# Two layers of a hybrid diffusion backbone on one core: loops written out as straight code, and two modulation jobs of the last layer left out

## What is computed

```python
def trunk_layer(x, m, latent, ...):
    h = rmsnorm(x, g[0]) * (1 + m[:, :, 0, 1]) + m[:, :, 0, 0]
    x = x + 0.5 * m[:, :, 0, 2] * rmsnorm(swiglu(h, wg[0], wu[0], wd[0]), g[1])
    h = rmsnorm(x, g[2]) * (1 + m[:, :, 1, 1]) + m[:, :, 1, 0]
    p = h @ w_in                       # Fourier | Hyena | q, k, v
    ...
    y = jnp.concatenate([y_f, y_h, y_a], axis=-1) @ w_out
    x = x + m[:, :, 1, 2] * rmsnorm(y, g[3])
    h = rmsnorm(x, g[4]) * (1 + m[:, :, 2, 1]) + m[:, :, 2, 0]
    x = x + 0.5 * m[:, :, 2, 2] * rmsnorm(swiglu(h, wg[1], wu[1], wd[1]), g[5])
```

## Time and profile before

| | |
|---|---|
| median of 3 runs | 1707.59 us (1707.35 to 1709.22) |
| span of the profiled execution, first to last instruction | 1706.8 us |
| mean granted TensorE clock | 0.985 |
| busy: PE, PEld | 1607.5 us, 1462.8 us |
| busy: DVE, ACT, POOL | 899.6 us, 765.5 us, 17.8 us |
| read from memory, written | 260.73 MB, 6.55 MB |

### The profile page before, as it was taken

One profiled execution on the slowest core, in us unless ns is written; L12 is line 12 of the kernel. 1 busy time (PEld: TensorE's weight loads), 2 busy tenths in 40 slices (PEclk: granted clock), 3 DMA queues, 4 the chain that ended last, 5 costly groups with the idle time before them and its releaser, 6 DMA issues.

```text
span 1706.8 us, 26956 instructions
## 1 busy us (share of the span) xinstructions
PE 1607.5 (94%) x9434; PEld 1462.8 (86%) x9434; DVE 899.6 (53%) x1597; ACT 765.5 (45%) x1176; POOL 17.8 (1%) x39
## 2 busy tenths in 40 slices
PE   6799999998988899999989999999898889999996
PEld 2399989996966699989979998999696669998996
DVE  5655544336685655544336554533667565554433
ACT  2355544325535555543255544432552555554332
POOL 0000000000000000000000000000000000000000
PEclk9999999999999999999999999999999999999998
DMA  6833685345501433474343368534550144337331
GB/s 232 333 107 125 249 294 182 130 159 182 181 1 38 173 123 123 137 282 138 129 167 100 124 247 293 191 124 165 181 181 1 36 163 130 124 126 298 132 124 65
DMA packets 70613, 268.20 MB, mean 157 GB/s; under 512 B 9387, under 2 KB 10444, under 8 KB 69900
## 3 DMA queue, kind: packets, MB, share of 16 engines
q1 hardware_dynamic: 67164, 248.96, 41.7%
q0 software_dynamic: 3376, 18.35, 2.8%
HBM read 260.73 MB, written 6.55 MB: 157 GB/s over the span
## 4 chain that ended last, share of the span: by engine, by line
PE 87%; DVE 6%; issue 3%; DMA 2%; ACT 2%; POOL 0%; DVEq 0%; SPq 0%; ACTq 0%; POOLq 0%
PE bank L529 26%; PE bank L531 25%; PE bank L530 25%; PE bank L538 4%; PE bank L867 1%; PE bank L829 1%; DVE y L1271 1%; DMA w_m<-w_mod 1%; DVE rstd L1266 1%; PE bank L753 1%; PE bank L617 1%; DMA f_cst<-tneg 1%; DVE sb_s L1457 1%; ACT prob_t L1068 1%; PE bank L856 1%
## 5 line engine op out<-in xcount | busy, mean ns | idle before, releaser
L1207 DVE TENSOR_TENSOR w_lo<-w_raw,w_hi 128x1024 fp32r<-128x1024 f32 (+2 forms) x288 | 373.6, 1297 | 527.5 <-ACT w_hi L927 526.6
L529 PE MATMUL bank<-h_hi,w_hi 128*128 128x386 f32 (+1 forms) x1760 | 606.3, 344 | 1.3 <-DVE w_lo L1207 0.8
L531 PE MATMUL bank<-h_hi,w_lo 128*128 128x386 f32 (+1 forms) x1760 | 596.1, 339 | 0.0
L530 PE MATMUL bank<-h_lo,w_hi 128*128 128x386 f32 (+1 forms) x1760 | 595.5, 338 | 0.0
L927 ACT ACTIVATE w_hi<-w_raw 128x1024 fp32r<-128x1024 f32 (+2 forms) x288 | 322.1, 1118 | 528.2 <-PE bank L531 527.6
L529 PEld LDWEIGHTS bank<-h_hi,w_hi 128*128 128x128 f32 x1760 | 332.0, 189 | 20.9 <-issue 14.0
L530 PEld LDWEIGHTS bank<-h_lo,w_hi 128*128 128x128 f32 x1760 | 332.8, 189 | 1.2
L531 PEld LDWEIGHTS bank<-h_hi,w_lo 128*128 128x128 f32 x1760 | 332.3, 189 | 0.0
L530 PE MATMUL bank<-hid_lo,w_hi 128*128 128x384 f32 x704 | 238.4, 339 | 0.0
L529 PE MATMUL bank<-hid_hi,w_hi 128*128 128x384 f32 x704 | 238.4, 339 | 0.0
L531 PE MATMUL bank<-hid_hi,w_lo 128*128 128x384 f32 x704 | 238.4, 339 | 0.0
(11 more groups left out here) (194 smaller groups left out, 1123.5 us busy)
## 6 DMA issues: line engine op xcount, KB each, us to landing
w_raw<-w_gu SPq DMA_DIRECT2D x176, 512.0 KB, 3.3
w_m<-w_mod SPq DMA_DIRECT2D x160, 512.0 KB, 6.3
w_raw<-w_dn SPq DMA_DIRECT2D x64, 704.0 KB, 4.0
w_raw<-w_in SPq DMA_DIRECT2D x26, 512.0 KB, 3.4
w_raw<-w_out SPq DMA_DIRECT2D x16, 512.0 KB, 3.4
cst<-consts POOLq DMA_DIRECT2D x8, 688.0 KB, 5.9
spec<-f_spec POOLq DMA_DIRECT2D x2, 2304.0 KB, 8.2
spc<-spec POOLq DMA_DIRECT2D x8, 576.0 KB, 5.1
```

The source lines that it names most:

```text
L529: mm(out, w_hi[:, wn, c], rhs_hi, start=first, stop=False)
L530: mm(out, w_hi[:, wn, c], rhs_lo, start=False, stop=False)
L531: return mm(out, w_lo[s][:, c], rhs_hi, start=False, stop=last)
L1207: TT(w_lo[unit % RAW][:, 0:n], w_raw[unit % RAW][:, 0:n], w_hi[:, unit % HIS, 0:n], ALU.subtract).then_inc(unit_lo.sem, 1)
```

## The change

All `Fori` loops become Python loops, so that each engine's program is straight code; the numbers to wait for and the addresses become constants. The last layer's feed-forward 1 gets no modulation jobs (`jobs_in`), and its norm's job is turned ahead of round 10 instead of round 8, since `first` is 10 there. `coefs(layer + 1, 0)` is not called in the last layer, and the third layer's room in `mod`, `bmod` and `vec` goes, with the two loads that filled it.

```diff
+def jobs_in(layer, n):
+
+    return 0 if n and layer == DEPTH - 1 else JOBS[n]
 ...
 class Steps:
     def at(self, n):
-        return self.layer * self.per_layer + (self.base + n)
+        return n
 ...
-        mod = sb("mod", [P, DEPTH + 1, NMOD * KT * 2])
-        bmod = sb("bmod", [P, (DEPTH + 1) * NMOD * KT])
+        mod = sb("mod", [P, DEPTH, NMOD * KT * 2])
+        bmod = sb("bmod", [P, DEPTH * NMOD * KT])
 ...
-                    sp.dma_start(vec[:, 0:DEPTH, :], vecs.rearrange("l p v -> p l v")).then_inc(vec_loaded.sem, 16)
-
-                    sp.dma_start(vec[:, DEPTH, :], vecs[DEPTH - 1]).then_inc(vec_loaded.sem, 16)
-                    sp.dma_start(bmod[:, 0:DEPTH * NMOD * KT], b_mod).then_inc(vec_loaded.sem, 16)
-                    sp.dma_start(bmod[:, DEPTH * NMOD * KT:],
-                                 b_mod[:, (DEPTH - 1) * NMOD * KT:]).then_inc(vec_loaded.sem, 16)
+                    sp.dma_start(vec[:, :, :], vecs.rearrange("l p v -> p l v")).then_inc(vec_loaded.sem, 16)
+                    sp.dma_start(bmod[:, :], b_mod).then_inc(vec_loaded.sem, 16)
 ...
-                with sp.Fori(1, first) as i:
+                for i in range(1, first):
                     gate_up(i)
-                gate_up(first, own=True)
-                with sp.Fori(first + 1, ROUNDS - 1) as i:
-                    gate_up(i, before=True, own=True)
-                gate_up(ROUNDS - 1, before=True)
+                for i in range(first, ROUNDS):
+                    gate_up(i, before=i > first, own=i < ROUNDS - 1)
 ...
             def ffn(layer, n):
-                first = ROUNDS - 1 - JOBS[n]
+                first = ROUNDS - 1 - jobs_in(layer, n)
 ...
-                with pe.Fori(1, first) as i:
+                for i in range(1, first):
                     body(i, False)
                 norm_job_turn(layer, 2 * n)
-                with pe.Fori(first, ROUNDS - 1) as i:
+                for i in range(first, ROUNDS - 1):
                     body(i, True)
 ...
-            with pe.Fori(0, DEPTH) as layer:
+            for layer in range(0, DEPTH):
                 ffn(layer, 0)
 ...
-                last = JOB_FFN[n] + JOBS[n] - 1
+                last = JOB_FFN[n] + jobs_in(layer, n) - 1
                 job_finish(layer * JL + (last + 3), layer * NMOD + (last + 2))
 ...
                 if n == 0:
                     coefs(layer, 1)
-                else:
+                elif layer + 1 < DEPTH:
                     coefs(layer + 1, 0)
```

More of the change, by code:

```diff
@@ L171, with __init__ @@
 class Steps:
-    def __init__(self, layer, per_layer, base=0):
-        self.layer, self.per_layer, self.base, self.n = layer, per_layer, base, 0
+    def __init__(self):
+        self.n = 0
     def step(self):
@@ L426, in round_job @@
                     else:
-                        job_loads(layer, i + (JOB_FFN[1] - first), DEPTH - 1, i - first, kts)
+                        job_loads(layer, i + (JOB_FFN[1] - first), layer + 1, i - first, kts)
                 def gate_up(i, before=False, own=False):
@@ L457, in _ @@
                 norm_loads(layer, 1, 1)
-                with sp.Fori(1, 3) as i:
+                for i in range(1, 3):
                     for u in range(4):
@@ L463, in _ @@
                     load_unit(layer, B_IN + 13 + j, w_in[layer, 13, :, a * P:b * P], (b - a) * P)
-                with sp.Fori(0, OUTT // 4) as i:
+                for i in range(0, OUTT // 4):
                     for u in range(4):
@@ L487, in _ @@
             pool.sem_inc(spec_free.sem, 1)
-            with pool.Fori(0, DEPTH) as layer:
+            for layer in range(0, DEPTH):
                 pool.wait_ge(spec_ready.sem, spec_ready.at(layer, 1))
@@ L699, in ffn @@
                     body(0, False)
-                with pe.Fori(1, first) as i:
+                for i in range(1, first):
                     body(i, False)
                 norm_job_turn(layer, 2 * n)
-                with pe.Fori(first, ROUNDS - 1) as i:
+                for i in range(first, ROUNDS - 1):
                     body(i, True)
                 body(ROUNDS - 1, False)
-                with pe.Fori(0, KT // 2) as i:
+                for i in range(0, KT // 2):
                     for u in range(4):
@@ L735, in project_in @@
                     tile_of(B_IN + u, u, 0, range(KT), True, True)
-                with pe.Fori(1, 3) as i:
+                for i in range(1, 3):
                     for u in range(4):
@@ L871, in project_out @@
             def project_out(layer):
-                with pe.Fori(0, OUTT // 4) as i:
+                for i in range(0, OUTT // 4):
                     for u in range(4):
@@ L907, in _ @@
             act.wait_ge(f_dec.sem, 1)
-            with act.Fori(0, DEPTH) as layer:
+            for layer in range(0, DEPTH):
                 act.wait_ge(f_hs.sem, f_hs.at(layer, 0))
@@ L981, in tile_steps @@
                       ACT.Copy).then_inc(hid_hi_done.sem, 1)
-                with act.Fori(0, ROUNDS - 1) as i:
+                for i in range(0, ROUNDS - 1):
                     tile_steps(i, 0)
@@ L1015, in centre @@
                       scale=vconv[:, 3 * i + 1:3 * i + 2]).then_inc(conv0.sem, 1)
-                with act.Fori(0, 2) as i:
+                for i in range(0, 2):
                     for u in range(4):
@@ L1124, in job_finish @@
                 TT(dst, src, bias.broadcast_to([P, 4, 2, 2]), ALU.add).then_inc(mod_ready.sem, 1)
-            ch = Steps(0, 0)
+            ch = Steps()
             for n in range(2):
@@ L1149, in _ @@
             STT(out=dec, in0=dec, scalar=-1.0, in1=dec, op0=ALU.mult, op1=ALU.max).then_inc(f_dec.sem, 1)
-            trace["dve_head"] = ch.n
-            with dve.Fori(0, DEPTH) as layer:
-                ch = Steps(layer, dve_steps[1], dve_steps[0])
+            for layer in range(0, DEPTH):
                 dve.wait_ge(f_win_done.sem, f_win_done.at(layer, 1))
@@ L1316, in tile_steps @@
                        ALU.subtract).then_inc(hid_lo_done.sem, 1)
-                with dve.Fori(0, first) as i:
+                for i in range(0, first):
                     tile_steps(i, 0, False)
                     tile_steps(i, 1, False)
-                with dve.Fori(first, ROUNDS - 1) as i:
+                for i in range(first, ROUNDS - 1):
                     tile_steps(i, 0, True)
                     tile_steps(i, 1, True)
-                last = JOB_FFN[n] + JOBS[n] - 1
+                last = JOB_FFN[n] + jobs_in(layer, n) - 1
                 job_finish(layer * JL + (last + 3), layer * NMOD + (last + 2))
@@ L1364, in scale @@
                     TT(prj[:, dst, PL], src[:, :, LAT], rs[:, :, LAT], ALU.mult).then_inc(in_scaled.sem, 1)
-                with dve.Fori(0, 2) as i:
+                for i in range(0, 2):
                     for u in range(4):
@@ L1505, in _ @@
             coefs(0, 0)
-            with dve.Fori(0, DEPTH) as layer:
-                ch = Steps(layer, dve_steps[2], dve_steps[0] + DEPTH * dve_steps[1])
+            for layer in range(0, DEPTH):
                 CP(vconv[:, :], vec[:, layer, V_CONV:V_CONV + 18]).then_inc(dve_step.sem, 1)
```

9 lines of the change are left out of this document (3 added, 6 removed).

## The result

The changed kernel takes 1689.15 us (median of 4 runs, 1688.4 to 1690.58) beside 1707.57 us of the kernel before on the same chip: ratio 0.989, 95% interval 0.9876 to 0.9904. The profiled execution, the slowest of the four, has a span of 1688.4 us, 18.4 under the one before.

The account below looks back on a forecast made before the run. PE was taken to bound the kernel, busy 94% of the span and full in the feed-forward rounds. Savings of 8.7 + 2.0 + 0.7 + 0.3 = 11.7 us, taken from the median 1707.59, gave 1696 us, range 1690 to 1700.5.

Parts of the forecast that it names:

- The jobs: Last layer's second feed-forward, rounds 8 and 9: dropping two modulation jobs at 4.3 us each on PE saves 8.7 us.
- rival D: Rounds that held the jobs: another engine is just behind PE, so their time is not given back; 1704 to 1707, chance 0.04.
- The turn of the layer: Layer loop's jump back: DVE's 3.05 us stall, taken as a wait for code, goes in straight code; gain 2.0 us.
- rival B: Turn of the layer: idle PE drops its clock, so the gain becomes a loss; 1699 to 1701 us, chance 0.17.
- The loops inside a stage: Rounds and down-projection: straight code saves no time, PE's queue covering branches; 97 us of ACT's table loads go.
- Rival A: Mixer stretches: half of the "issue" time is register work, giving 6.4 us where 0.3 is counted; 1690, chance 0.12.
- an estimate of 1689 us: All 64 PE loop ends at about 108 ns each, 6.9 us more saved; the prediction held nearly all these branches hidden.
- The head: Filter loop before the rounds: 0.5 us at the turn between passes and 0.2 for small steps, 0.7 us saved.
- Code fetch: PE's full stretches: more instruction packets expected for straight code, but no gaps on PE inside rounds.
- rival C: PE's full stretches: straight code is fetched anew each round and arrives late, 107 us more, 1803; chance 0.03.
- Smaller loads and the last coefficients: Two duplicate loads (73 KB) and two short DVE instructions go, all off the path: nothing gained.

Follow-up runs that it names:

- the second trace: The changed kernel unchanged, run again on the chip of the last two follow-up runs: 1688.65 us, ratio 0.9886 to the kernel before.

## Why the prediction came out as it did

**The jobs: right.** Forecast 8.7, measured 8.6 against before (8.3 in the second trace) and 8.75 between the two kernels that differ by the jobs and what goes with them. The half job's 2.06 us from the earlier trace rows (2.05 by those rows) and the turn's 0.2 from the earlier trace rows carried it. Nothing was late behind PE, so rival D did not happen: DVE and ACT, at half load, had the room that was claimed.

**The turn of the layer: right, with part of rival B in it.** DVE, then PE, in the changed kernel:

```profile
886.14 0.96 DVE L1252 TENSOR_TENSOR x<-x,y 128x768 f32<-128x768 f32 x1
887.13 0.18 DVE L1486 COPY vconv<-vec 128x18 f32<-128x18 f32 x1
```

```profile
873.56 0.34 PE L513 MATMUL bank<-hid_hi,w_lo 128*128 128x384 f32 x1
...
875.32 1.93 PE L520 MATMUL bank<-w_m,csil 128*32 128x256 f32 x32
882.45 5.79 PE L604 MATMUL bank<-xsq,ones 128*128 128x384 f32 x12 [5.19 <-ACT xsq L925]
...
890.28 1.93 PE L520 MATMUL bank<-w_m,csil 128*32 128x256 f32 x32
892.15 0.44 PE L511 MATMUL bank<-h_hi,w_hi 128*128 128x386 f32 x1
...
896.51 0.34 PE L511 MATMUL bank<-h_hi,w_hi 128*128 128x386 f32 x1
```

The stretches there, columns as in the earlier trace rows:

```profile
880.00:882.00 2.00, 0.00 (x0) 0.00 (x0) 1.97 (x3) 0.45 (x1) 0.00 (x0) 0.96 0.99 385
882.00:884.00 2.00, 1.55 (x3) 0.95 (x4) 1.97 (x3) 2.00 (x6) 0.00 (x0) 0.50 0.43 174
884.00:886.00 2.00, 2.00 (x6) 1.09 (x5) 1.97 (x3) 2.00 (x6) 0.00 (x0) 0.68 0.00 0
886.00:888.00 2.00, 2.00 (x7) 0.73 (x5) 1.78 (x5) 2.00 (x6) 0.00 (x0) 1.00 0.00 0
```

The 3.05 us gap of the earlier trace rows is gone. In the kernel before, an instruction queue moved packets during that gap (891.59 to 894.65):

```profile
q14 instruction: 3, 0.02, 2.1%
```

In the changed kernel neither instruction queue moved one from 862 to 889. That fits the prediction's reading of the gap, a wait for code at the jump back; that the packets were DVE's is not shown. The second unit starts at 896.51, 23.0 us after the last down-projection matmul, as forecast, where it was 25.0. PE did run its rows early and then stood idle for 5.19 us, and its clock fell to 0.50, the lower level, as rival B said. But it was back at 1.00 by 886 to 888, and the second half of the rows at 890.28 took 1.93 us, the value of the full clock and not the 3.64 of the earlier trace rows. The condition of rival B, a clock still low at 893, was not met. The 2.0 is read from the stages of the traces; straight code alone, head and turn together, gave the whole kernel 0.3 to 3.6 us.

**The loops inside a stage: right.** Writing them out moves the time by a factor of 0.9996 to 1.0015. ACT lost 103 us of busy time in the changed kernel and nothing followed. Its first full stretch, beside the first line of the earlier trace rows:

```profile
100.00:380.00 280.00, 279.72 (x1759) 269.81 (x1758) 129.40 (x224) 99.29 (x140) 0.00 (x0) 1.00 0.52 186
```

The 0.28 us that PE lacks is a wait for a load of modulation weights. Rival A (half of the mixers' "issue", 6 us) did not happen: the first mixer stretch, from the input projection's last matmul to the output projection's first, takes 73.9 us before and 73.8 after, the second 75.5 and 75.4.

By the Trainium skill, Advanced Engine Details and Errata, section Control Flow Timing, the prediction had an estimate of 1689 us, which is the time that came. It came for another reason: the kernel with the inner loops written out has lost 60 of PE's 64 loop ends, by the Trainium skill's 108 ns an estimate of 6.5 us, and is not faster. A time that agrees shows nothing about the mechanism.

**The head: right in kind, but mis-sized: 0.7, and it measured 1.9.** I costed the turn between the two passes at 0.5 and the small steps at 0.2. PE's first transform of each pass, in the changed kernel:

```profile
24.45 1.12 PE L561 MATMUL bank<-f_s,f_cst 128*128 128x512 f32 x2
...
49.21 1.13 PE L561 MATMUL bank<-f_s,f_cst 128*128 128x512 f32 x2 [0.78 <-DVE f_f L1150]
```

With the filter loop kept they start at 25.43 and 50.88, in the kernel before at 25.25 and 51.09. So 0.8 to 1.0 us is gone ahead of the first transform, where the loop is entered, a step that I had not looked at, and another 0.7 to 1.1 in the second pass. (In the straight kernels here the first transform starts anywhere from 23.90 to 24.87 us; that the loop's entry is what costs the first part is argued from its place.) The last load of modulation weights did move up, the condition that I had put.

**Code fetch: right.** The queue that had moved 35 packets moved 73 (rival C's premise), and PE stays full in the rounds. The Trainium skill, Advanced Engine Details and Errata, section ISA Cache, was weighed there at a chance of 0.03; no run here shows an engine out of code within straight code.

**The step that failed** is the one of *Smaller loads and the last coefficients*, with its result "Nothing". I followed the shrunken tensors as loads and as instructions and never as a layout. They stand in front of most other tiles, and two of those, `hid_hi` and `hid_lo`, are read by 2112 matmuls, back to back, in stretches where PE is the only bound. That was worth 7.0 us: without it the kernel takes 1697.0, within 1 us of the forecast (its trace has 2.2 for the head, 2.1 for the turn, 8.5 for the jobs and 0.3 more for all else: 12.4 by the spans, 11.2 by the medians, where 11.7 was forecast). A hint stood in the trace of before: with PE full and the clock at 1.00, the steps of the down-projection went through 174, 180, 175 and 177 ns over and over; in the changed kernel they are 173 and 174.

## What to carry to other kernels

Where a stretch is bound by one engine without a gap, ask also for the step of its instructions, and list every tile that an edit moves in memory: a smaller tensor can change the pace of matmuls that the edit never touches. Test such a cause by moving the tile and nothing else (an unused tile as padding), and enter each setting of a probe in several ways before trusting one sample. In this kernel loop ends, registers and table loads under a full engine cost nothing that could be measured (ratio 0.9996 to 1.0015); what gave time were the filter loop in the head (1.9 us) and the turn of the layer loop (2.0), where the other engines wait too.

## What the runs showed of the hardware that I had not expected

- The step of back-to-back matmuls with a new weight load each depends on how the moving columns lie to the weights in a partition: 173.3 or 176.6 ns at 384 columns for two starts 128 bytes apart, swapped by moving the weights 128 bytes; up to 179.5 at other starts; 173.3 to 180.0 at 386 columns. The granted clock was at 1.00. The commonest steps, 173.3, 176.7 and 180.0 ns, are 416, 424 and 432 cycles at 2.4 GHz.
- At some distances the same code holds 173 or 180 ns for whole stretches, by how it enters them (two entries against four of six at a start of 96).
- 386 columns can run at the 173.3 ns of 384.
